# A hybrid attention/mLSTM encoder step: decays made once per chunk, chunk loads on another queue, and finer waits ahead of one projection panel

## What is computed

```
z = h @ w_in          # q_A k_A v_A | q_B k_B v_B | i_B f_B | o_B | gate_A gate_B
ya = local_attention(q_A, k_A, v_A)
yb = sigmoid(o_B) * head_norm(mlstm(q_B, k_B, v_B, i_B, f_B))
merged = sigmoid(gate_A) * (ya @ w_proj_a) + sigmoid(gate_B) * (yb @ w_proj_b)
x = layer_norm(alpha*x + g1 * (merged @ w_out))
x = layer_norm(alpha*x + g2 * conv_ffn(x*(1+sc2)+sh2))
```

```
b = cumsum(fc)                                       # fc: log forget gates
dmat = where(causal, b[l] - b[s] + ic[s], -inf)      # ic: input gates
inter = b + m
m_t = maximum(max(dmat, -1), inter)
w = exp(dmat - m_t)          ;  g = exp(inter - m_t)
s = (q @ k.T) * w
num = s @ v + g * (C @ q)    ;  den = sum(s) + g * (n @ q)
h = num / maximum(abs(den), exp(-m_t))
wk = exp(b[-1] - b + ic - m_new)  ;  decay = exp(b[-1] + m - m_new)
C = decay * C + (wk * v) x k ;  n = decay * n + wk x k
```

## Time and profile before

| what | before |
|---|---|
| median of 3 runs (lowest, highest) | 1966.47 us (1966.08, 1966.5) |
| the profiled execution | 1964.41 us |
| its span in the trace | 1962.6 us |
| PE, DVE, ACT, POOL busy in it | 1893.6, 1057.4, 622.7, 561.5 us |

### The profile page before, as it was taken

The page is one execution under the profiler, slowest core; times in us unless marked ns, Lnnn a source line. Parts: engine busy times, 40 slices in busy tenths (PEclk is TensorE's granted clock), DMA queues, the critical chain, the costliest instruction groups (busy, mean ns, idle before and its releaser), DMA issues.

```text
span 1962.6 us, 29540 instructions
## 1 busy us (share of the span) xinstructions
PE 1893.6 (96%) x11935; PEld 1824.1 (93%) x11935; DVE 1057.4 (54%) x1886; ACT 622.7 (32%) x1409; POOL 561.5 (29%) x312
## 2 busy tenths in 40 slices
PE   7997999999999999999899999999999999999995
PEld 6997988887999999979899989999999999999995
DVE  5897554446333333463344687564455536444487
ACT  2113454453232232351311255222223222222333
POOL 2432212112222222122234445233223323322330
PEclk9998999999999999999999999999999999999997
...
DMA packets 74185, 171.41 MB, mean 87 GB/s; under 512 B 8496, under 2 KB 37680, under 8 KB 73920
## 3 DMA queue, kind: packets, MB, share of 16 engines
...
...
## 4 chain that ended last, share of the span: by engine, by line
PE 82%; DVE 11%; ACT 2%; DVEq 2%; issue 1%; DMA 1%; ACTq 1%; SPq 0%
PE acc L413 29%; PE px L686 16%; PE acc L686 10%; PE px L696 7%; DVE adaT_tmp L1225 5%; PE acc L696 4%; PE px L663 2%; PE px L478 2%; PE acc L663 1%; PE px L500 1%; PE px L497 1%; PE px L580 1%; PE px L582 1%; PE px L581 1%; DMA ada_ring<-in_w_ada 1%
## 5 line engine op out<-in xcount | busy, mean ns | idle before, releaser
L413 PE MATMUL acc<-x_hilo_a,w_hilo 128*128 128x352 f32 x4176 | 725.0, 329 | 9.7 <-DVE x_c L1427 6.0
L413 PEld LDWEIGHTS acc<-x_hilo_a,w_hilo 128*128 128x128 f32 x4176 | 673.5, 189 | 27.0 <-issue 16.3
L378 POOL CAST w_hilo<-w_raw 128x1024 fp32r<-128x1024 f32 x133 | 147.3, 1108 | 1235.9 <-PE acc L413 691.9
L380 POOL TENSOR_TENSOR w_hilo<-w_raw,w_hilo 128x1024 fp32r<-128x1024 f32 x133 | 347.2, 2611 | 10.6
L686 PE MATMUL px<-x_hilo_a,w_hilo 128*128 128x352 f32 x1968 | 319.1, 322 | 0.0
L686 PEld LDWEIGHTS px<-x_hilo_a,w_hilo 128*128 128x128 f32 x1968 | 315.3, 188 | 0.5 <-issue 0.5
L686 PE MATMUL acc<-x_hilo_a,w_hilo 128*128 128x352 f32 x1200 | 194.2, 321 | 0.0
L686 PEld LDWEIGHTS acc<-x_hilo_a,w_hilo 128*128 128x128 f32 x1200 | 191.4, 188 | 0.0
L696 PE MATMUL px<-ffn_act,w_hilo 128*128 128x352 f32 x864 | 146.1, 323 | 0.0
L696 PEld LDWEIGHTS px<-ffn_act,w_hilo 128*128 128x128 f32 x864 | 140.2, 189 | 0.2
L1102 ACT ACTIVATE u_rows<-px,ffn_consts 128x352 f32<-128x352 f32 (+2 forms) x110 | 49.5, 478 | 238.4 <-PE px L686 238.4
...
## 6 DMA issues: line engine op xcount, KB each, us to landing
...
```

The lines of the kernel that those rows point to most:

```text
L378: nc.gpsimd.tensor_copy(to[:, 0, :], raw[:, s, :]).then_inc(w_hi, 1)
L380: nc.gpsimd.tensor_tensor(to[:, 1, :], raw[:, s, :], to[:, 0, :].bitcast(F32), ALU.subtract).then_inc(w_ready, 1)
L413: last = mm(acc[:, n, 0:NW], whl[:, slot, wi, k * P:(k + 1) * P], rhs[:, xi, k, n * NW:(n + 1) * NW], start=(k == 0 and j == 0), stop=(k = ...
```

## The change

Three things change together.

1. **Decays per chunk.** The broadcast matmul L570 and DVE's copy L1365 go. `rowR` is stored to a DRAM tensor (`r_spill`) once, and the four rows of a chunk are loaded from there by a transfer that repeats them on all partitions, into rows 2 and 3 of `stage` (views `gb` and `wd`, one of each for even and for odd chunks). DVE makes both exponents for all four heads in three operations (`exponents`), ACT both exponentials in two (`decays`), DVE the scaled queries in one (`queries`). `exponents(c+1)` and `decays(c+1)` stand in unit h = 3 of chunk c, `queries(c)` at the head of unit h = 0.
2. **Chunk loads.** `zc` and the broadcast rows are loaded on SP's queue, behind the panel four ahead of the chunk's first; each load waits for `e_done`, the end of the chunk before the last. The first one also stores `rowR` and waits for it.
3. **First branch panel.** Its matmuls wait tile by tile (`ya_lo`, KT*n+k+1), and ACT rounds the first four tiles of n = 0 one unit earlier.

The core of the diff:

```diff
+            def load_chunk(c):
+                L, par = (LC, c % 2) if c < NLC else (TS, 0)
+                tok = slice(c * LC, c * LC + L)
+                if c == 0:
+                    sp.wait_ge(rr_rdy, 1)
+                    sp.dma_start(io["rr"], rowR[:, :]).then_inc(rr_out, 16)
+                    sp.wait_ge(o_used, 2 * NCH + 2)
+                    sp.wait_ge(kv_out, 16 * 8)
+                    sp.wait_ge(sp_out[0], 16 * 9)
+                    sp.wait_ge(sp_out[1], 16 * 8)
+                    sp.wait_ge(rr_out, 16)
+                wait(sp, e_done, 4 * c - 4)
+                sp.dma_start(gb[par][:, :, 0:L], io["rr"][:, tok].unsqueeze(0).to_broadcast([P, HB, L])).then_inc(rb_in[par], 16)
+                sp.dma_start(zc[:, par, :, 0:L], io["zs"][1:17, :, tok].rearrange("q p t -> p q t")).then_inc(zc_in[par], 16)
+
+            chunk_after = {P_ML + 3: 0}
+            for c in range(NLC):
+                chunk_after[P_ML + ml_part(c)[0] + 4] = c + 1
             for p in range(4, N_PANEL):
                 panel(p)
+                if p in chunk_after:
+                    load_chunk(chunk_after[p])
...
-                mm(px[0:L, 0, 0:L], z[:, h, 0:L], z[:, 4 + h, 0:L], start=True, stop=True)
-                tok = slice(c * LC, c * LC + L) if isinstance(c, int) else bass.ds(c * LC, L)
-                mm(px[:, 0, P:P + L], sel[:, h, :], rowR[:, tok], start=True, stop=True).then_inc(sr_rdy, 1)
+                mm(px[0:L, 0, 0:L], z[:, h, 0:L], z[:, 4 + h, 0:L], start=True, stop=True).then_inc(sr_rdy, 1)
...
+                if h == 0:
+                    pe.wait_ge(qg_rdy, c + 1)
...
+            pe.wait_ge(w_ready, P_PA + 1)
             for n in range(NT):
-                pe.wait_ge(ya_lo, KT * (n + 1))
-                gemm(P_PA, SLOT[P_PA], n, XA)
+                pe.wait_ge(acc_free[n], P_PA)
+                for k in range(KT):
+                    pe.wait_ge(ya_lo, KT * n + k + 1)
+                    for j, (wi, xi) in enumerate(((0, 0), (0, 1), (1, 0))):
+                        last = mm(acc[:, n, 0:NW], whl[:, SLOT[P_PA], wi, k * P:(k + 1) * P], XA[:, xi, k, n * NW:(n + 1) * NW],
+                                  start=(k == 0 and j == 0), stop=(k == KT - 1 and j == 2))
+                last.then_inc(acc_ready[n], 1)
...
+            def decays(c):
+                L, par = (LC, c % 2) if c < NLC else (TS, 0)
+                act.wait_ge(d_rdy, c + 1)
+                A(wd[par][0:L, :, 0:L], wd[par][0:L, :, 0:L], ACT.Exp)
+                A(gb[par][:, :, 0:L], gb[par][:, :, 0:L], ACT.Exp).then_inc(wg_rdy, 1)
+                act.wait_ge(wg_rdy, c + 1)
+                A(wks[0:L, par, :], wd[par][0:L, :, L - 1], ACT.Copy, scale=KB_SCALE).then_inc(wk_rdy, 1)
...
-                act.wait_ge(d_rdy, u + 1)
-                A(wd[0:L, 0:L], wd[0:L, 0:L], ACT.Exp)
-                bias = mp_c[:, h, c:c + 1] if isinstance(c, int) else mp_c[:, h, bass.ds(c, 1)]
-                A(gb[:, 0:L], rs[:, 0:L], ACT.Exp, bias=bias).then_inc(wg_rdy, 1)
-                act.wait_ge(wg_rdy, u + 1)
-                A(wks[0:L, :], wd[0:L, L - 1:L], ACT.Copy, scale=KB_SCALE)
+                if h == 0:
+                    act.wait_ge(wk_rdy, c + 1)
                 act.wait_ge(kvt_rdy, u + 1)
                 wait(act, nu_rdy, u)
                 A(va[0:L, 0:DV], px[0:L, 1, P:3 * P], ACT.Copy)
-                act.drain()
-                A(kw[0:L, :], px[0:L, 1, 0:P], ACT.Copy, scale=wks[0:L, :]).then_inc(kv_rdy, 1)
+                A(kw[0:L, :], px[0:L, 1, 0:P], ACT.Copy, scale=wks[0:L, par, h:h + 1]).then_inc(kv_rdy, 1)
...
-                if h == 1 and not smp:
-                    wait(act, nu_rdy, c * 4)
-                    load_chunk(c + 1, 1 - par, TS if isinstance(c, int) and c == NLC - 1 else LC)
                 if smp and h == HB - 1:
-                    ya_round(0)
+                    ya_round(0, range(4, KT))
                 if h == 3:
+                    if not smp:
+                        decays(c + 1)
...
+                if smp and h == HB - 2:
+                    ya_round(0, range(4))
...
+            def exponents(c):
+                L, par = (LC, c % 2) if c < NLC else (TS, 0)
+                dve.wait_ge(rb_in[par], 16 * (c // 2 + 1))
+                V.tensor_tensor(wd[par][0:L, :, 0:L], gb[par][0:L, :, 0:L], at_c[0:L, c, :].unsqueeze(2).to_broadcast([L, HB, L]), ALU.add)
+                dve.drain()
+                V.tensor_tensor(wd[par][0:L, :, 0:L], wd[par][0:L, :, 0:L], cmask[0:L, 0:L].unsqueeze(1).to_broadcast([L, HB, L]), ALU.add)
+                V.tensor_tensor(gb[par][:, :, 0:L], gb[par][:, :, 0:L], mp_c[:, :, c].unsqueeze(2).to_broadcast([P, HB, L]), ALU.add)
+                dve.drain().then_inc(d_rdy, 1)
+
+            def queries(c):
+                L, par = (LC, c % 2) if c < NLC else (TS, 0)
+                dve.wait_ge(wk_rdy, c + 1)
+                dve.wait_ge(zc_in[par], 16 * (c // 2 + 1))
+                V.tensor_tensor(qg[:, par, :, 0:L], zc[:, par, 4:8, 0:L], gb[par][:, :, 0:L], ALU.mult).then_inc(qg_rdy, 1)
...
+                    queries(c)
                 dve.wait_ge(sr_rdy, u + 1)
-                V.tensor_copy(rs[:, 0:L], px[:, 0, P:P + L])
-                dve.drain()
-                V.scalar_tensor_tensor(wd[0:L, 0:L], rs[0:L, 0:L], col(at_c), cmask[0:L, 0:L], ALU.add, ALU.add).then_inc(d_rdy, 1)
-                dve.wait_ge(wg_rdy, u + 1)
-                V.scalar_tensor_tensor(pt[0:L, 0:L], px[0:L, 0, 0:L], KB_SCALE, wd[0:L, 0:L], ALU.mult, ALU.mult)
-                V.tensor_tensor(qg[:, 0:L], zc[:, par, 4 + h, 0:L], gb[:, 0:L], ALU.mult)
-                dve.drain().then_inc(p_rdy, 1)
+                V.scalar_tensor_tensor(pt[0:L, 0:L], px[0:L, 0, 0:L], KB_SCALE, wd[par][0:L, h, 0:L], ALU.mult, ALU.mult).then_inc(p_rdy, 1)
...
+                if h == HB - 1 and ci != NLC:
+                    exponents(c + 1)
```

30 lines of the change are left out of this document (14 added, 16 removed).

## The result

| what | before | after |
|---|---|---|
| median (lowest, highest), 4 runs each | 1966.49 us (1966.08, 1967.48) | 1939.38 us (1938.50, 1940.02) |
| the profiled execution | 1964.41 us | 1939.18 us |
| its span | 1962.6 us | 1937.3 us |
| PE, DVE, ACT, POOL busy in it | 1893.6, 1057.4, 622.7, 561.5 us | 1872.9, 1051.0, 604.4, 564.1 us |

After over before is 0.9866, with a 95% interval from 0.9854 to 0.9878: 27.1 us less. Direction and mechanism were right, and one term was too small. Medians and differences here are of runs in the fast state; one slow run of before, at 10611 us, is left out.

A forecast was written before the change was run, and what follows sets the result against it. The prediction took PE, busy throughout the middle of the mLSTM stage, as the bound. Its terms, 14.6 + 2.9 - 0.6 - 0.4 + 5.3 = 21.8 us, off 1966.47 gave 1944.7 us, range 1941.5 to 1950.5.

The forecast's parts named there:

- 1a, the matmul's slot: mLSTM units: removing 36 broadcast matmuls takes 0.42 us each off PE, 0.31 for four short ones; 14.6 us gained.
- the edges: Heads of chunks: queries ahead of p_t make PE late at three short edges, 0.2 us each; 0.6 us lost.
- The rival of this step: Weight loads of the transposes behind take part of the 0.42; half of 14.6 lost, 1952.0 us; chance 0.04.
- 1b, the five waits: PE's five short waits at or just behind heads of chunks in the mLSTM stage go; 2.9 us gained.
- The first unit: First mLSTM unit: queries held up by GpSimd make p_t end late; 0.4 us lost.
- Part 2: Chunk loads moved to SP's queue: the delay to panels hides and ScalarE's relief gains nothing; 0 us.
- Part 3: First branch panel: tile-by-tile waiting removes PE's 3.34 us wait and the half clock behind it; 5.3 us gained.
- The wait of 0.7 at the turn: Behind the first branch panel, PE would stand 0.7 us for the normed rows of the last chunk.
- The wait further on: mLSTM branch, at 940.04: PE's 4.96 us wait for loads and elementwise work moves with the turn and stays as long.
- the rival in which the branch's chain doesn't move: The wait at 940.04 grows from 4.96 to 10.3 us; 5.3 lost, 1950.0 us; chance 0.07.

The follow-up runs named there:

- experiment 4: The kernel before with its broadcast matmul replaced by one of 128 rows, copy and exponentials left as they are: 1953.70 us, ratio 0.9944.
- Experiment 8: The changed kernel with VectorE making the queries four times instead of once at the head of each chunk: 1952.67 us.
- experiment 1: A second profile of each kernel, before and changed, both unchanged: 1965.83 and 1938.23 us.

## Why the prediction was right or wrong

- **1a, the matmul's slot: the step that failed.** The forecast took the start of the broadcast matmul to the start of the next, 0.42, as all that leaves, and named 0.42 x 36 as the upper bound. The neighbours' distances, 0.31 and 0.16, were in the very same timeline, and it took them for the normal pace of such a pair. There was a row to hold against it: the next two transposes stand 0.11 apart (665.89 and 666.00), not 0.16. Measured 19.2 instead of 14.6, by the timelines and by putting the matmul back (19.3). The matmul itself needs only 0.22 of the 0.56; the other 0.34 is the price of going from full-row matmuls to a 4-row one and back, which the forecast didn't have. This 4.6 is nearly the whole miss of 5.3; the edges make 0.6 of it. The rival of this step (the slot not all saved) had the wrong sign.
- **1b, the five waits:** all gone, 2.9 as forecast. They were one kind of wait, and taking the chain out of the unit removed them. Shortening PE's list alone doesn't: it made four of them 0.34 longer each (experiment 4).
- **The edges:** 0 instead of 0.6. The room was counted right (2.2 us at the short ones), and the block by GpSimd, which the forecast set against it, falls elsewhere in the changed kernel. Experiment 8 shows what it costs when it doesn't.
- **The first unit:** 0.35 for 0.4, by the reason given (the queries beside GpSimd's subtraction, 1.74 us).
- **Part 2:** the price against the kernel before was right, 0, in the two profiles of after (no wait of PE names a load); in four of the kernels made from it PE waits 0.21 to 0.75 us for `c_state` (experiment 1). The reason was thin. The forecast compared with a queue that carries one load a chunk; part 1 adds a second, and on ScalarE's queue the two would have cost 9 to 10 us of the 22. It is what makes part 1 worth its price, though it saves nothing by itself.
- **Part 3:** 5.35 for 5.3, with the clock at 1.00 through the 48 matmuls. The wait of 0.7 at the turn didn't come: PE waited 0.38 at the head of the 48 matmuls, was held to VectorE's pace and reached the turn at 862.30, right at the end of the normed rows. The sum of both is the same.
- **The wait further on** stayed at 4.96, as forecast, and the rival in which the branch's chain doesn't move is out.
- **The sum:** 19.2 + 2.9 - 0.35 + 5.35 = 27.1. The range's lower end was made of the upper bounds of the terms; since the bound of the largest one was no bound, the range missed.
